# Laying out the on-chip buffers anew: what TensorE reads begins at multiples of 2 KB

## What is computed

```
# first block, twice
x = x + 0.5 * swiglu_ffn(rmsnorm(x, ffn1_norm), ffn1_wi, ffn1_wo)      # 1024 -> 2 * 2816 -> 1024
z = rmsnorm(x, mix_norm) @ w_in
hA = mlstm_chunkwise(...); hB = swa_sink_attention(...)
mixed = sigmoid(ga) * ((sigmoid(mo) * rmsnorm(hA)) @ w_a) + sigmoid(gb) * (hB @ w_b)
x = x + mixed @ w_out
x = x + 0.5 * swiglu_ffn(rmsnorm(x, ffn2_norm), ffn2_wi, ffn2_wo)
x = x + sigmoid(rmsnorm(x, ple_norm) @ w_ple_gate) * (p @ w_ple)
# second block, twice
proj = rmsnorm_2(x, norm_mix_g) @ w_in
mix = concat(gmlp_mixer(uv, ..., gmlp_b_s), ssd_mixer(z, xbc, dt, ...), mla_mixer(...))
x = x + mix @ w_out
x = x + square(relu(rmsnorm_2(x, norm_mlp_g) @ mlp_w1)) @ mlp_w2       # 1024 -> 4096 -> 1024
```

## Time and profile before

| | |
|---|---|
| median of 3 runs | 3871.23 us (3866.43 to 3871.86) |
| profiled execution, span of its instructions | 3867.6 us |
| what lies around the span, median less span | 3.6 us |
| TensorE matmuls | 3661.1 us busy, 15582 |
| VectorE / ScalarE / POOL | 1841.0 / 1006.2 / 1404.7 us busy |
| mean granted TensorE clock | 0.964 of full speed |

### The profile page before, as it was taken

One profiled execution on the slowest core, in us unless ns is written; L12 is line 12 of the kernel. 1 busy time (PEld: TensorE's weight loads), 2 busy tenths in 40 slices (PEclk: granted clock), 3 DMA queues, 4 the chain that ended last, 5 costly groups with the idle time before them and its releaser, 6 DMA issues.

```text
span 3867.6 us, 44550 instructions
## 1 busy us (share of the span) xinstructions
PE 3661.1 (95%) x15582; PEld 2828.9 (73%) x15582; DVE 1841.0 (48%) x2258; ACT 1006.2 (26%) x1320; POOL 1404.7 (36%) x581
## 2 busy tenths in 40 slices
PE   3999999999999999999999999898899999889997
PEld 2888865778887788875678888664688876467886
DVE  3542224754424542323665422757463554748163
ACT  1222223322222222222422222333221123322111
POOL 1444432334443444331234443321244432114442
PEclk6999999999999999999999999888999998899998
DMA  3332321223322332231223323211133231113231
GB/s 92 106 98 93 96 68 49 71 82 98 98 97 86 96 96 94 84 90 44 66 78 101 98 98 96 71 32 30 54 104 97 94 87 37 36 44 91 94 98 60
DMA packets 473852, 309.79 MB, mean 80 GB/s; under 512 B 16809, under 2 KB 432531, under 8 KB 473715
## 3 DMA queue, kind: packets, MB, share of 16 engines
q1 hardware_dynamic: 470224, 305.16, 26.4%
q10 hardware_dynamic: 3491, 2.80, 0.5%
HBM read 304.25 MB, written 3.67 MB: 80 GB/s over the span
## 4 chain that ended last, share of the span: by engine, by line
issue 65%; POOL 24%; PE 9%; POOLq 1%; DVE 0%; ACT 0%; DVEq 0%
POOL wl L421 24%; PE bank L444 2%; PE bank L443 2%; PE bank L439 2%; PE bank L462 1%; PE bank L458 1%; PE bank L464 1%; POOLq L420 0%; POOLq L418 0%; PE bank L465 0%; DVE y_sb L2014 0%; PE mb L503 0%; DVE var L1444 0%; DVE var L1424 0%; POOLq L421 0%
## 5 line engine op out<-in xcount | busy, mean ns | idle before, releaser
L421 POOL TENSOR_TENSOR wl<-raw,wh 128x1024 fp32r<-128x1024 f32 x576 | 1404.3, 2440 | 2413.1 <-ACT wh L1093 2412.8
L1093 ACT ACTIVATE wh<-raw 128x1024 fp32r<-128x1024 f32 x576 | 607.1, 1056 | 1626.0 <-PE bank L458 793.6
L458 PE MATMUL bank<-xh,wh 128*128 128x512 f32 x2528 | 995.9, 394 | 3.5 <-DVE xl L1418 3.5
L462 PE MATMUL bank<-xl,wh 128*128 128x512 f32 x2528 | 990.2, 392 | 0.0
L464 PE MATMUL bank<-xh,wl 128*128 128x512 f32 x2212 | 866.5, 392 | 0.0
L458 PEld LDWEIGHTS bank<-xh,wh 128*128 128x128 f32 x2528 | 478.4, 189 | 119.3 <-issue 18.5
L462 PEld LDWEIGHTS bank<-xl,wh 128*128 128x128 f32 x2528 | 478.7, 189 | 99.2
L444 PE MATMUL bank<-hh,wl 128*128 128x512 f32 (+1 forms) x1216 | 485.1, 399 | 0.0
L464 PEld LDWEIGHTS bank<-xh,wl 128*128 128x128 f32 x2212 | 418.8, 189 | 88.8
L443 PE MATMUL bank<-hl,wh 128*128 128x512 f32 (+1 forms) x1216 | 479.2, 394 | 0.0
L439 PE MATMUL bank<-hh,wh 128*128 128x512 f32 (+1 forms) x1216 | 476.8, 392 | 0.0
(11 more groups left out here) (358 smaller groups left out, 3439.5 us busy)
## 6 DMA issues: line engine op xcount, KB each, us to landing
raw<-in_ffn_wi_dram SPq DMA_DIRECT2D x176, 512.0 KB, 3.8
raw<-in_mlp_w_dram SPq DMA_DIRECT2D x128, 512.0 KB, 3.8
raw<-in_w_in_dram SPq DMA_DIRECT2D x102, 512.0 KB, 3.7
raw<-in_ffn_wo_dram SPq DMA_DIRECT2D x88, 512.0 KB, 3.6
raw<-in_w_out_dram SPq DMA_DIRECT2D x32, 512.0 KB, 3.9
raw<-in_w_ple_gate_dram SPq DMA_DIRECT2D x16, 512.0 KB, 3.6
raw<-in_w_a_dram SPq DMA_DIRECT2D x8, 512.0 KB, 3.5
raw<-in_w_b_dram SPq DMA_DIRECT2D x8, 512.0 KB, 3.4
```

Source lines behind the costliest of these rows:

```text
L421: gp.tensor_tensor(wl[j][:], raw[j % RAW_SLOTS][:], wh[j][:].bitcast(F32), ALU.subtract)\
L458: first = pe.matmul(out[0:width, :], h[:, c:c + width], rh[:, k, :], start=k == 0, stop=False)
L462: pe.matmul(out[0:width, :], h[:, c:c + width], rl[:, k, :], start=False, stop=False)
L1093: act.activation(wh[n % SPLIT_SLOTS][:], raw[n % RAW_SLOTS][:], ACT.Copy).then_inc(s.hi_ready, 1)
```

## The change

No buffer changes its size or its use. Their places change:

- The small tables that no matmul reads (`par2`, `p2`, `first_gains`, `small`, `p1` and others) and `bs_now` go to the bytes from 16512 up to 9 x 2048 = 18432. `x_sb` begins there, and `xh`, `xl`, the slabs, the scratch rows, `const` and `ones` follow as before. Each is a multiple of 2 KB long up to `const`.
- `const` loses a block: the 32 columns of `C_SEL` go into the unused part of the rotation's block.
- `gate_h`, `gate_l`, `gate_raw`, `sel4` of the first block share their bytes with `bs_rows`, `a_col`, `dt_col` of the second. `bias`, `rope` and the region begin at 63 x 2048 and later multiples.
- As `bs_rows` now lies where the first block's gate weights are, it is loaded by SP between the blocks, behind `rope`, with a semaphore of its own, and VectorE waits for it.

Offsets, from adding up the sizes in the order of `place`:

| buffer | before | past a multiple of 2048 | after | past a multiple of 2048 |
|---|---|---|---|---|
| `x_sb` | 16512 | 128 | 18432 | 0 |
| `xh` / `xl` | 32896 / 49280 | 128 | 34816 / 51200 | 0 |
| `wh0` / `wl0` | 73856 / 90240 | 128 | 75776 / 92160 | 0 |
| `const` (identity first) | 120960 | 128 | 122880 | 0 |
| `ones` | 126080 | 1152 | 126976 | 0 |
| region: `hh`, `proj`, `q96` | 139232 | 2016 | 137216 | 0 |
| `hl` | 184288 | 2016 | 182272 | 0 |
| `mh` / `ml` | 163808 / 139232 | 2016 | 161792 / 137216 | 0 |
| `gv_sq` | 212960 | 2016 | 210944 | 0 |

The diff, cut to its core:

```
-C_IDENT, C_SEL, C_DUP0, C_DUP1, C_MQS, C_MSQ, C_ROT, C_TRI, C_BACK = [P * n for n in range(9)]
-CONSTS = 9 * P
+C_IDENT, C_ROT, C_DUP0, C_DUP1, C_MQS, C_MSQ, C_TRI, C_BACK = [P * n for n in range(8)]
+C_SEL = C_ROT + MLA_D
+CONSTS = 8 * P
...
+        par2 = place("par2", [P, R2])
+        p2 = place("p2", [P, 2 * R2 + KT])
...
+        bs_now = place("bs_now", [4, P], offset=cursor[0])
+        p1 = place("p1", [P, 2 * R1])
+        par1 = place("par1", [P, R1])
+        assert cursor[0] <= 9 * 2048, cursor[0]
+        cursor[0] = 9 * 2048
         x_sb = place("x_sb", [P, KT, S])
...
+        union = cursor[0]
         gate_h = place("gate_h", [P, KT, 8], F32R)
         gate_l = place("gate_l", [P, KT, 8], F32R)
+        gate_raw = place("gate_raw", [P, KT, 8])
+        sel4 = place("sel4", [ML_H, P])
+        bs_rows = place("bs_rows", [4, 2, P], offset=union)
...
+        cursor[0] = 63 * 2048
         bias_at = cursor[0]
         bias = place("bias", [P, SW_H, 2 * P])
         rope = place("rope", [MLA_D, 2, S], offset=bias_at)
         region = cursor[0]
+        assert region % 2048 == 0
...
             sp.dma_start(rope[:], a["rope_pack"]).then_inc(s.rope_landed, 16)
+
+            sp.dma_start(bs_rows[:], a["gmlp_b_s_2"].rearrange("l h t -> h l t")).then_inc(s.bs_landed, 16)
...
-                act.dma_start(bs_rows[:], a["gmlp_b_s_2"].rearrange("l h t -> h l t")).then_inc(s.setup_small, 16)
...
+                dve.wait_ge(s.bs_landed, 16)
                 dve.tensor_copy(bs_now[:, None, :], bs_rows[:, bass.ds(L, 1), :])
```

More of the change, by code:

```diff
@@ L121, in sem @@
             return ctx.enter_context(nc.semaphore(name))
+        par2 = place("par2", [P, R2])
+        p2 = place("p2", [P, 2 * R2 + KT])
+        first_gains = place("first_gains", [P, 5 * KT])
+        small = place("small", [P, 64])
+        g_first = small[:, 48:48 + KT]
+        d_skip = place("d_skip", [P, 2, 3])
+        d_skip_now = place("d_skip_now", [P, 3])
+        dt_bias = place("dt_bias", [SSD_H, 2])
+        dt_a = place("dt_a", [SSD_H, 2])
+        dt_now = place("dt_now", [SSD_H, 2])
+        b_gate = place("b_gate", [ML_H, 2, 2])
+        b_gate_now = place("b_gate_now", [ML_H, 2])
+        sinks = place("sinks", [P, 2, SW_H])
+        sinks_now = place("sinks_now", [P, SW_H])
+        bs_now = place("bs_now", [4, P], offset=cursor[0])
[3 more added lines that the diff above has]
+        cursor[0] = 9 * 2048
         x_sb = place("x_sb", [P, KT, S])
@@ L135, in program @@
         const = place("const", [P, CONSTS])
-        sel4 = place("sel4", [ML_H, P])
         ones = place("ones", [P, P])
[L138 to L143, removed]
+        union = cursor[0]
         gate_h = place("gate_h", [P, KT, 8], F32R)
         gate_l = place("gate_l", [P, KT, 8], F32R)
[L146 to L149, removed]
-        c_col = place("c_col", [P, NT, ML_H])
[L151 to L161, removed]
+        gate_raw = place("gate_raw", [P, KT, 8])
+        sel4 = place("sel4", [ML_H, P])
+        bs_rows = place("bs_rows", [4, 2, P], offset=union)
+        a_col = place("a_col", [P, NT, SSD_H], offset=union + 1024)
+        dt_col = place("dt_col", [P, NT, SSD_H], offset=union + 1024 + 96)
+        c_col = place("c_col", [P, NT, ML_H])
+        assert cursor[0] <= 63 * 2048 and union + 1280 <= cursor[0]
+        cursor[0] = 63 * 2048
         bias_at = cursor[0]
@@ L265, in program @@
             sp_ready y_psum y_done y_squared y_ss y_inv y_rs y_bc y_bc_read y_scaled y_rounded ssd_done
-            c_squared c_ss c_inv c_rs c_bc c_scaled c_split rope_landed rot_psum rot_read rot_done
+            c_squared c_ss c_inv c_rs c_bc c_scaled c_split rope_landed bs_landed rot_psum rot_read rot_done
             kv_done key_rows vt_psum vt_copied al_ready am_ready ae_ready ap_ready at_ready at_copied ao_ready ao_done
@@ L2024 @@
 ML_OFF = [0, 512, 896, 1152]
-N_SMALL = 11 + 1 + 4 + 2 + 4 + 2 + 2 + 1
+N_SMALL = 11 + 1 + 4 + 2 + 4 + 1 + 2 + 1
 def constants(np):
```

## The result

| | before | after |
|---|---|---|
| median of the runs made side by side | 3869.7 us (3866.43 to 3871.86, 4 runs) | 3833.0 us (3830.81 to 3836.32, 4 runs) |
| ratio, 95% interval | | 0.9908 [0.9894, 0.9922] |
| span of the profiled execution | 3867.6 us | 3834.5 us |
| mean granted TensorE clock | 0.964 | 0.966 |

What follows compares the result with a forecast made beforehand. TensorE was taken as the bound, by the pitch of its gapless matmuls. Four items at 215.8 ns a matmul gave 161 us: 3867.6 - 161 + 3.6 = 3710 us, range 3690 to 3875 (forecast's own 3690 to 3785).

Steps and rivals of the forecast that it cites:

- The step that failed: Inference that the 2 KB boundary crossing itself causes the 13.3 and 20 ns excess in full-rate f32r matmuls.
- The aligned pitch: Start-to-start time of 512-column f32r matmuls without a crossing, taken as 215.8 ns; bounds 215.8 and 237.5 ns.
- Item 1: Dense xh matmuls in input projections, gate and second block's MLP: 6970 x 10.9 ns = 76 us gained.
- Item 2: Matmuls over hh, hl, where TensorE has no gap: 3648 x 17.5 ns = 63.8 us gained.
- Item 3: The 864 matmuls over hah, hbh, pth, mh, ml: 14.7 us at 17 ns, taken as 9 us.
- Item 4: Remaining 1920 xh matmuls filling gaps in recurrences and attention: 25 us, of which half, 12 us, was taken.
- Setup, 0.3 us: Setup may end 0.3 us sooner, as issuing bs_rows leaves ScalarE's queue ahead of the load it ends on.
- Only the early crossing costs: Rival: xh keeps 226.7 ns, only hh and the like come down to it; 29 us gained, 3842 us; chance 0.22.
- Nothing happens: Rival: pitch goes by where in memory a buffer lies, not by its offset; 3871 us; chance 0.14.
- The start is the worst place: Rival: alignment leaves no column ahead of the boundary, all matmuls go at 237.5 ns; 3974 us; chance 0.10.
- whether VectorE keeps up at 216 ns: Second block's MLP: VectorE keeps up by 0.3 us a tile; if not, 16.7 us of gain would be lost.
- Reading (c): Weight load length isn't the cause: with 4 stationary columns xh matmuls take 232 ns, no less than 226.7.

Runs made afterwards that it cites:

- both_32: Changed kernel with xh, xl, slabs, const, ones and the whole region all beginning 32 bytes past a 2 KB multiple; 3835.3 us, ratio 0.9916 to the kernel before.
- x_32: Changed kernel with x_sb, xh, xl, slabs, scratch rows, const and ones 32 bytes past a 2 KB multiple, region unmoved; 3864.7 us, ratio 0.9990 to the kernel before.
- before_pad: Kernel before with const packed into 8 blocks and 160 empty bytes ahead of the region; 3837.2 us, ratio 0.9921 to the kernel before.
- bf16: Changed kernel with bfloat16 hh, hl and upper halves of wh, wl as bfloat16 weights in the down projections, so less exact; 3799.1 us.
- region_32: Changed kernel with only the region (hh, mh and others) beginning 32 bytes past a 2 KB multiple; 3865.8 us, ratio 0.9996 to the kernel before.
- stat_64: Changed kernel using 64 of 128 stationary columns in the down projections, half of each result left out; 3848.2 us.
- same_column: Changed kernel whose down projections send the first position's column 512 times (step 0), so products hold one position's values; 3795.8 us.

## Why the prediction was wrong

**What bounds the kernel.** Right. TensorE had no gap in the dense streams and has none now, and the time went down by what their pitch went down.

**The step that failed** is the one from "it depends on the place of the crossing" to "it is the crossing", in the words of the forecast: "the excess moves with the place of the crossing and with nothing else that I can find". There was something else. The streams of the earlier trace rows differ in where the moving buffer lies; but the slabs lie at 128 in both, so they differ in the distance to the slabs too: 0 in the one and 1888, which is 96 past a multiple of 256, in the other. A trace of one layout holds place and distance together. `both_32` and `x_32` take them apart: crossing in every matmul at 226.7 ns, and a stream that crosses nothing at 233.3. And where the crossing lies is nothing either: after 480 columns in the earlier trace rows, 504 in `both_32`, 96 in `before_pad`, always 226.7.

**The aligned pitch.** Taken as 215.8, measured 226.7. The f32 passes of the earlier trace rows were the nearest rows but not near: at half the column rate the fixed cost doesn't show, and this says nothing on what of it a full-rate matmul owes to its place. The Trainium skill (TensorE: Matmul & The Clock Gate, Back-to-back issue gap) gives N/2.4 + 2.5 ns as the gap of a matmul by itself, by which 512 columns are an estimated 215.8 ns. By the runs this holds for the stream of `bf16`, 215.5, and not for the f32r matmuls of this kernel in any layout tried, 226.7 at best.

**The terms of the sum.** Item 1, dense `xh`, 76 us: 0. Item 2, `hh`, 63.8 us: 24.4, as each matmul fell by 6.7 ns and not by 17.5. Item 3, the 864, 9 us: 3.8 in `hah`, `hbh` and `mh`, 0.7 in `pth`. Item 4, mixed `xh`, 12 us: none by its pitch, and 2.5 us scattered over those stages with no cause shown, less than two runs of one kernel can differ by. Setup, 0.3 us: the dense part starts 1.7 us sooner, but this start lies anywhere from 83.0 to 86.3 us in the spans of the experiments, and at 83.8 in `before_pad`, which has the old load. I don't count it as the change's.

The measured 3833 us lie within the range of 3690 to 3875 only because that was stretched over the rivals; the forecast's own range ended at 3785.

**The rivals.** "Only the early crossing costs" gave 3842 us, and its numbers came: `xh` keeps 226.7, `hh` comes down to it, the floor is 226 or more. Its mechanism is as wrong as the forecast's: in `region_32` the crossing is late and the stream pays in full. Whoever had taken it would have been right by luck. What is true in it is that 13.3 ns stay at every distance tried. "Nothing happens" fell with the groups over `hh`, and so did its cause, the absolute place: `both_32` and `before_pad` have every buffer within some hundred bytes of where slow kernels have them. "The start is the worst place" fell with the first start over `xh`.

**What was said to cost nothing** cost nothing: VectorE and POOL have the busy time of before in the second block's MLP (68.83 and 38.13 of 76.60 us), whose pitch didn't change, so the question whether VectorE keeps up at 216 ns was never put. The moved load and its wait are hidden as worked out. Reading (c) holds too: `stat_64` confirms that a shorter weight load isn't a shorter matmul, as the earlier trace rows had it, and `both_32`, in which one weight tile in four crosses a 2 KB boundary, that such a crossing is nothing. But the 232 ns of the earlier trace rows say more than reading (c) took from them: with 4 stationary columns the pitch is 231 to 232 ns in every layout, 226.7 in none.

**What stays open.** Which part of the chip makes the pitch go by the remainder of the two addresses, why 64 costs a third of what 32 and 128 do, and why fewer than 128 stationary columns make the pitch longer. The runs show the rule, not the part. Nor do they tell whether a matmul's own weights count or those of the next one, which load while it streams (in the timeline a load starts 0.23 us ahead of its matmul): all tiles of the slabs have one remainder. The scratch rows and `const` keep their distance to the slabs in every layout; TensorE doesn't read them in these streams, and VectorE is busy for 21.59 of 119.68 us while every matmul has its pitch, which speaks against them, but no run shows it. The remainder 160 and distances off the grid of 32 bytes weren't tried, nor a `bf16` stream at a bad distance, nor an f32r stream whose weights stay. `same_column` changes the address pattern and the number of bytes read at once, and `bf16` the type and the bytes of both operands, so that they don't tell which of these carries the 13.3 ns.

## What to carry to other kernels

Where f32r matmuls with 128 stationary columns follow each other without a gap, compare the pitch of streams of the same shape over different buffers; if one is dearer, put its moving buffer and its weights at the same remainder to 256 bytes, which a few empty bytes do, and look for no alignment beyond that. When a trace shows that a cost goes with an operand's address, write down the addresses of all operands of both streams before naming a cause: one layout can't tell a place from a distance, and one kernel with everything shifted alike can. The distance between starts is the measure for such a stream; busy time and the mean of one instruction hardly moved (392 to 389 ns).

## What the hardware showed that I had not expected

- A 512-column f32r matmul with 128 stationary columns takes 226.7 ns from start to start when moving and stationary addresses agree modulo 256 bytes, 228.9 at remainder 64, 232.4 to 233.3 at 32, 96, 128, 192 and 224, at the full granted clock of 2.4 GHz. A 2 KB boundary inside the operand costs nothing (`both_32`, 119.68 us for 528).
- At the best distance 13.3 ns over the bare columns stay at 512 columns and 13.4 at 384. They fall to 3.2 with a moving operand of step 0 and to 2.2 in bfloat16.
- With 64 stationary columns the pitch rises from 226.7 to 230.0 ns; with 96 and with 4 it is 231 to 232 in every layout.
